# A wait ahead of the gathers of the final sum: until the last chunk of the last expert's weights is in SBUF

## Chip, cores and metric

The kernel runs on one core of one Trainium2 chip. The metric is the device time of one execution in microseconds (us); lower is better. Engines are named as in the profile: PE is TensorE's matmuls and PEld its weight loads, DVE is VectorE, ACT ScalarE, POOL GpSimd, SP SyncE.

## What is computed

One layer of a diffusion backbone on 384 tokens (128 context tokens, 256 latent tokens, D_MODEL 1024): a token mixer, then a mixture of 32 experts in which each token goes to four of them, then the final RMSNorm. The part that the change touches is the end of the routed layer and its sum:

```python
def routed_ffn(h, lp):                       # h: 384 x 1024, TOP_K = 4, 32 experts
    logits = (h @ lp["w_router"] + lp["b_router"]).astype(jnp.float32)
    top_val, top_idx = lax.top_k(logits, TOP_K)
    gates = jax.nn.softmax(top_val, axis=-1)
    ...
    def run_block(args):
        xb, e = args
        hb = xb @ w1[e] + b1[e]
        glu, lin = jnp.split(hb, 2, axis=-1)
        glu = jnp.minimum(glu, SWIGLU_LIMIT)
        lin = jnp.clip(lin, -SWIGLU_LIMIT, SWIGLU_LIMIT)
        act = glu * jax.nn.sigmoid(SWIGLU_ALPHA * glu) * (lin + 1.0)
        return act @ w2[e] + b2[e]
    ys = lax.map(run_block, (xs, block_e)).reshape(cap, d_model)
    return jnp.zeros_like(h).at[slot_t].add(ys * slot_g[:, None].astype(ys.dtype))

x = x + g2 * routed_ffn(h.reshape(B * T, D), lp).reshape(B, T, D)
y_prompt, y_sample = rmsnorm(x_ctx, norm_f), rmsnorm(x_lat, norm_f)
```

Everything is float32.

## The kernel before, in words

The program is written by hand, engine by engine: each engine has one list of instructions (`@block.sync`, `@block.gpsimd`, `@block.tensor`, `@block.scalar`, `@block.vector`), which it runs in the order written, and counting semaphores tie the lists together. Compute instructions add 1 to a semaphore and a DMA adds 16 when it has landed.

**Expert stage.** The tokens of each expert are cut into blocks of HB = 64 rows; here there are 39 blocks, one iteration each on PE, ACT, DVE and POOL, and the last of them is number `last_it` and belongs to expert 31. An expert's weights are 12 MB, in WC = 12 chunks of 1 MB: chunks 0 to 7 from `w_moe_in`, 8 to 11 from `w_moe_out`. SP issues them (line 569), expert after expert, each as soon as its buffer is free, and each chunk position c has a semaphore of its own, `s_es[c]`, which has reached 16·(e+1) when chunk c of expert e is in. Chunks 0 to 3 land in four staging buffers (two in `ring`, two in `work`), from which DVE copies them on (line 1852); chunks 4 to 7 (tile `work`) and 8 to 11 (tile `ring`) are multiplied where they land. PE multiplies in order (all matmuls have line 689): chunks 0 to 7, then, after the activation on DVE and ACT, chunks 8 to 11. At the end of every block but the last, ACT takes the 64 x 1024 result out of PSUM bank 2 and writes it to the DRAM tensor `rows_d` with two DMAs (line 1393), which count on semaphore `yo`.

**Last block.** Its result stays in PSUM. During it, ACT loads the norm gains and the modulation rows (lines 1366 to 1372; the tiles `smallw`, `first`, `work`; semaphore `cons3`).

**The gathers.** After its share of the blocks POOL waits until `rows_d` is written (`yo`, line 670), and until DVE has copied the last block's chunks 0 to 3 out of the staging buffers (`stg`, line 672), runs a tiny operation to hold its place (line 673), and issues 12 indirect DMAs (line 678). Each gathers 128 rows of 4 KB from `rows_d`, one per token, by the index column `dest[:, n]`: numbers 0 to 3 for token tile 0 (into `ring`), 4 to 7 for tile 1 (into `work`), 8 to 11 for tile 2 (into `zbuf`, after PE has multiplied chunks 0 to 3, lines 676 and 677). The semaphore `s_yg[j]` has reached 64 when tile j's four gathers have landed.

**The sum.** DVE's list after the last block (lines 1896 to 1911) is: `gathered(0)`, `gathered(1)`, two products of the last block's rows with the modulation gate (`ysc`, line 1901, which wait for PE's last multiplication and for the rows that ACT loads), `gathered(2)`, then `summed(j)`, `mean_square(j)` and `final_norm(j)` for the three tiles. `gathered(j)` waits for `s_yg[j]`, scales tile j's first gathered rows by the gate (line 1874) and adds the other three (line 1876):

```python
            def gathered(j):
                ve.wait_ge(s_yg[j], 16 * TOPK)
                L(ts(facc[j], facc[j], early[:, j, 0:1], None, M))
                for k in range(1, TOPK):
                    L(stt(facc[j], ygat[TOPK * j + k], early[:, j, k:k + 1], facc[j], M, A_))
```

PE puts the residual x1 into six banks after its last expert chunk (12 matmuls on `ky` and `ident`), and adds the last block's rows when `ysc` is there (12 matmuls on `work`, 64 rows). `summed(j)` adds a bank to tile j, ACT squares it, POOL takes the root (line 683), DVE scales (line 1894), and SP stores the tile (line 597).

Of the kernel before, what the change touches and what calls it, by code (L numbers as in the profile page):

```python
# [39 lines left out]
NE = 32  # L40
# [41 lines left out]
WC = W1C + W2C  # L82
# [60 lines left out]
def build(nc, a, o):  # L143
    ctx = ExitStack()
    with ctx:
# [46 lines left out]
        def at(buf, start, *shape, rows=P):  # L192
            n = int(np.prod(shape))
            v = buf[0:rows, start:start + n]
            if len(shape) == 1:
                return v
            names = "abcd"[:len(shape)]
            return v.rearrange(f"p ({' '.join(names)}) -> p {' '.join(names)}",
                               **{names[i]: shape[i] for i in range(len(shape))})
# [141 lines left out]
        s_es = [sem(f"s_es{i}") for i in range(WC)]  # L341
# [261 lines left out]
        @block.gpsimd  # L603
        def _(gp):
            gp.memset(at(ky, 0, D), 0.0).then_inc(S["gpn"], 1)
            gp.memset(half[:, :], -0.5).then_inc(S["gpn"], 1)
            gp.wait_ge(S["gpn"], 2)
            rs = ALU.pow
            for j in range(NT):
                gp.wait_ge(S["ssq"], j + 1)  # L610
                gp.tensor_tensor(stat[:, 8 + j:9 + j], stat[:, 4 + j:5 + j], half[:, 0:1], rs).then_inc(S["rstd"], 1)
            for j in range(NT):
                gp.wait_ge(S["anorm"], j + 1)
                gp.tensor_tensor(stat[:, 36:46], stat[:, 26:36], half[:, 0:10], rs).then_inc(S["arstd"], 1)  # L614
            for j in range(NT):
                gp.wait_ge(S["kkss"], j + 1)
                gp.tensor_tensor(stat[:, 16:24], stat[:, 8:16], half[:, 0:8], rs).then_inc(S["kkr"], 1)

            def rest_of_bias(i):
                rows = slice((0, 2 * NE)[i], QMAX)  # L620
                gp.wait_ge(S["kkr"], NT + i + 2)
                gp.wait_ge(S["b3d"], (1, 4)[i])
                gp.tensor_tensor(bias32[rows, :], bias32[rows, :], b3[rows, :], ALU.subtract).then_inc(S["b3d"], 1)  # L623

            for j in range(NT):
                gp.wait_ge(S["kkss"], NT + j + 1)
                if j == 2:
                    gp.wait_ge(S["b3d"], 2)
                gp.tensor_tensor(stat[:, 16:24], stat[:, 8:16], half[:, 0:8], rs).then_inc(S["kkr"], 1)
                if j:  # L630
                    rest_of_bias(j - 1)
            gp.wait_ge(S["b3d"], 5)
            for j in range(NT):
                gp.wait_ge(S["ssq"], NT + j + 1)
                gp.tensor_tensor(stat[:, 8 + j:9 + j], stat[:, 4 + j:5 + j], half[:, 0:1], rs).then_inc(S["rstd"], 1)

            def gather_rows():
                gp.indirect_dma_start(xg, None, h2_d.rearrange("t (h n) -> (t h) n", h=2), bass.IndirectOffsetOnAxis(ap=slots[:, 0:1], axis=0))\
                  .then_inc(S["xgd"], 16)

            def gather_first():
                gp.wait_ge(S["idxc"], 1)
                gp.wait_ge(S["h2out"], 16 * NT)
                gp.tensor_tensor(half[:, 12:13], half[:, 13:14], half[:, 13:14], ALU.mult).then_inc(S["gpn"], 1)
                gather_rows()

            def gather_listed(it):
                gp.wait_ge(S["idxc"], 2)
                gp.wait_ge(S["xgd"], 16 * it + 16)
                gp.wait_ge(S["gpn"], 3 * it + 3)  # L650
                gp.tensor_tensor(half[:, 12:13], half[:, 13:14], half[:, 13:14], ALU.mult).then_inc(S["gpn"], 1)  # L651
                gp.tensor_copy(slots[:, 0:1], lists[:, bass.ds(it + 1, 1)]).then_inc(S["gpn"], 1)
                gp.wait_ge(S["gpn"], 3 * it + 5)
                gp.tensor_tensor(half[:, 14:15], half[:, 13:14], half[:, 13:14], ALU.mult).then_inc(S["gpn"], 1)
                gather_rows()

            gather_first()
            gp.wait_ge(S["routeq"], 8)
            last_it = gp.value_load(tab[0:1, LAST:LAST + 1], min_val=NE - 1, max_val=NBMAX - 1)

            def block_of(it, last):
                if not last:
                    gp.wait_ge(S["xtm"], it + 1)
                    gather_listed(it)

            with gp.Fori(0, last_it) as it:
                block_of(it, False)
            block_of(last_it, True)

            gp.wait_ge(S["yo"], 32 * last_it + 32)  # L670
            gp.wait_ge(S["gpn"], 3 * last_it + 3)
            gp.wait_ge(S["stg"], NST * last_it + 2 * NST)
            gp.tensor_tensor(half[:, 12:13], half[:, 13:14], half[:, 13:14], ALU.mult)
            for n in range(NT * TOPK):
                if n == 2 * NST:
                    gp.wait_ge(S["mult"], WC * last_it + (NST + ZQ_ALL))
                    gp.tensor_tensor(half[:, 15:16], half[:, 13:14], half[:, 13:14], ALU.mult)
                gp.indirect_dma_start(ygat[n], None, rows_d,
                                      bass.IndirectOffsetOnAxis(ap=dest[:, n:n + 1], axis=0))\
                  .then_inc(s_yg[n // TOPK], 16)  # L680
            for j in range(NT):
                gp.wait_ge(S["ssq"], 2 * NT + j + 1)
                gp.tensor_tensor(stat[:, 8 + j:9 + j], stat[:, 4 + j:5 + j], half[:, 0:1], rs).then_inc(S["rstd"], 1)
# [1256 lines left out]
```

## Time and profile before

| | us |
|---|---|
| median of 3 runs | 1818.67 |
| the three runs | 1815.39, 1818.67, 1831.9 |
| the profiled execution | 1815.35 |
| its span, first to last instruction | 1813.5 |
| mean granted TensorE clock in it | 0.926 of full |

The profile is of one execution of its own, so its times are set against 1815.35 us. Stretches are in microseconds from the span's start. In the chain of waits each row is a start, a length, and the work, DMA or queue that the end of the program waited for at that point. In a timeline a row is one instruction or several of a kind: start, time from its start to the end of the last, engine, line, operation, tiles written and read, count, and in brackets how long the engine was idle before it and what ended that. A POOL row of a gather shows the making of the DMA's descriptors, not the moving of its data. "DMA" in a row of stretches is the mean busy share of the core's 16 DMA engines. Queue q1 is SP's, q10 is ACT's and q0 is POOL's.

### The profile page before, as it was taken

What the parts mean: (1) busy time and instruction counts of PE and PEld (TensorE: products, weight loads), DVE (VectorE), ACT (ScalarE), POOL (GpSimd) and SP (SyncE); (2) the same over time, 40 slices, a digit from 0 to 9 for tenths busy, and PEclk for the clock granted to TensorE, in tenths of its full rate; (3) what the DMA queues carried; (4) which work ended last, traced back from release to release, by engine and by line L of the source; (5) the groups of instructions that cost most, each with busy time, mean ns of one, the idle gap of its engine ahead of it and who ended that gap; (6) DMA issues with size and microseconds to landing.
All of it is one profiled execution on the core that took longest, in us unless ns stands there. A gap on an engine that the chain in (4) does not pass through costs nothing.

```text
span 1813.5 us, 28729 instructions
## 1 busy us (share of the span) xinstructions
PE 1540.9 (85%) x11145; PEld 749.4 (41%) x11146; DVE 702.4 (39%) x1093; ACT 260.1 (14%) x508; POOL 109.0 (6%) x194
## 2 busy tenths in 40 slices
PE   2699959598998996999997878999888889878974
PEld 0588825497895453333332222233222233222321
DVE  1433255777676445333322222233222232222316
ACT  0233313202212100111110101011101011001101
POOL 0000010100002100000000000000000000000020
PEclk8799968699998985999999998999999999999988
DMA  8534472300006462987799999978999989999895
GB/s 340 206 103 158 172 304 91 141 4 8 3 4 193 168 236 104 395 352 287 287 421 422 421 422 422 377 300 365 422 421 422 421 334 419 421 422 406 366 412 229
DMA packets 98524, 516.90 MB, mean 285 GB/s; under 512 B 13880, under 2 KB 16200, under 8 KB 45752
## 3 DMA queue, kind: packets, MB, share of 16 engines
q1 hardware_dynamic: 81928, 480.88, 65.8%
q10 hardware_dynamic: 11680, 18.49, 2.8%
q0 software_dynamic: 4848, 16.52, 2.5%
q8 instruction: 56, 0.92, 0.2%
q14 instruction: 12, 0.10, 0.0%
HBM read 493.12 MB, written 22.72 MB: 284 GB/s over the span
## 4 chain that ended last, share of the span: by engine, by line
PE 53%; DMA 31%; DVE 9%; issue 3%; POOL 2%; ACT 1%; SPq 0%; DVEq 0%; ACTq 0%; POOLq 0%
PE bank L689 51%; DMA work<-w_moe_in 26%; PE bank L696 2%; DMA work<-rows_d,dest 1%; DMA ring<-w_ada 1%; DVE work L1863 1%; DVE work L1597 1%; DMA work<-mods_d 1%; DMA work<-b_moe_out 1%; DVE work L1864 1%; DVE work L1606 0%; DMA rows_d<-work 0%; DVE work L1690 0%; POOL work L623 0%; POOL stat L614 0%
## 5 line engine op out<-in xcount | busy, mean ns | idle before, releaser
L689 PE MATMUL bank<-work 64*64 64x64 f32 (+3 forms) x5468 | 486.2, 324 | 79.1 <-DMA work<-w_moe_in 72.9
L689 PE MATMUL bank<-ring,work 128*64 128x512 f32 (+1 forms) x1440 | 364.2, 598 | 11.7 <-ACT work L1175 5.7
L689 PEld LDWEIGHTS bank<-work 64*64 64x64 f32 (+2 forms) x5468 | 240.0, 139 | 315.3 <-issue 161.8
L689 PE MATMUL bank<-zbuf,work 128*64 128x512 f32 (+2 forms) x1560 | 267.5, 451 | 25.0 <-DVE zbuf L1852 24.8
L689 PEld LDWEIGHTS bank<-ring,work 128*64 128x64 f32 (+1 forms) x1440 | 123.1, 145 | 220.5 <-issue 205.8
L1175 ACT ACTIVATE work<-bank 128x512 f32<-128x512 f32 (+3 forms) x227 | 112.7, 514 | 635.5 <-PE bank L689 344.9
L1857 DVE TENSOR_SCALAR work<-bank 128x512 f32<-128x512 f32 x39 | 27.0, 692 | 452.2 <-PE bank L689 452.2
L689 PEld LDWEIGHTS bank<-zbuf,work 128*64 128x64 f32 (+2 forms) x1560 | 110.4, 142 | 173.0 <-issue 106.4
L689 PE MATMUL bank<-parts 128*128 128x512 f32 (+1 forms) x720 | 158.0, 382 | 3.4 <-DVE parts L420 3.4
L696 PE MATMUL bank<-ident,work 128*128 128x128 f32 (+2 forms) x407 | 83.0, 322 | 73.2 <-DVE work L1443 21.7
L689 PEld LDWEIGHTS bank<-parts 128*128 128x128 f32 x720 | 131.5, 191 | 29.9 <-issue 3.4
L1852 DVE COPY zbuf<-work 128x2048 f32<-128x2048 f32 x78 | 94.1, 1224 | 64.7 <-DMA work<-w_moe_in 62.4
L1376 ACT ACTIVATE work<-work 128x512 f32<-128x512 f32 x39 | 24.6, 630 | 564.6 <-DVE work L1857 564.6
L696 PEld LDWEIGHTS bank<-ident,work 128*128 128x128 f32 (+2 forms) x407 | 56.0, 177 | 114.3 <-DVE work L1864 33.9
L1852 DVE COPY first<-ring 128x2048 f32<-128x2048 f32 x39 | 47.9, 1227 | 125.0 <-DMA ring<-w_moe_in 104.4
L420 DVE TENSOR_TENSOR parts<-ring,parts 128x1024 fp32r<-128x1024 f32 (+1 forms) x40 | 45.7, 1146 | 103.9 <-ACT parts L415 103.9
L689 PE MATMUL bank<-first,work 128*64 128x512 f32 x312 | 75.9, 607 | 10.4 <-DVE first L1852 10.4
L651 POOL TENSOR_TENSOR half<-half 128x1 f32<-128x1 f32 x38 | 7.5, 198 | 946.0 <-PE bank L696 935.2
L1852 DVE COPY zbuf<-ring 128x2048 f32<-128x2048 f32 x39 | 47.6, 1222 | 25.2 <-DMA ring<-w_moe_in 25.2
L1863 DVE TENSOR_SCALAR work<-bank 128x256 f32<-128x256 f32 x78 | 32.8, 420 | 62.7 <-PE bank L689 62.7
L415 ACT ACTIVATE parts<-ring 128x1024 fp32r<-128x1024 f32 (+1 forms) x40 | 39.8, 999 | 102.2 <-PE bank L689 102.2
L689 PE MATMUL bank<-ring,condT 128*2 128x512 f32 x192 | 32.6, 790 | 19.2 <-DMA ring<-w_ada 18.3
(234 smaller groups left out, 890.1 us busy)
## 6 DMA issues: line engine op xcount, KB each, us to landing
work<-w_moe_in SPq DMA_DIRECT2D x192, 1024.0 KB, 21.5
ring<-w_moe_out SPq DMA_DIRECT2D x128, 1024.0 KB, 23.3
ring<-w_moe_in SPq DMA_DIRECT2D x64, 1024.0 KB, 22.1
ring<-w_ada SPq DMA_DIRECT2D x12, 2048.0 KB, 8.6
ring<-w_in SPq DMA_DIRECT2D x9, 2048.0 KB, 8.1
rows_d<-work ACTq DMA_DIRECT2D x76, 128.0 KB, 6.6
rows_d<-ky SPq DMA_DIRECT2D x11, 512.0 KB, 15.0
ring<-w_out SPq DMA_DIRECT2D x2, 2048.0 KB, 12.9
```

The source lines that it names most:

```text
L415: nc.scalar.activation(zpart(t, 0, n), z_quarter(t), ACT.Copy).then_inc(S["hi"], 1)
L420: eng.tensor_tensor(zpart(t, 1, n), z_quarter(t), zpart(t, 0, n), ALU.subtract)\
L651: gp.tensor_tensor(half[:, 12:13], half[:, 13:14], half[:, 13:14], ALU.mult).then_inc(S["gpn"], 1)
L689: return pe.matmul(out, l, r, start=start, stop=stop)
L696: return pe.transpose(out, src, ident[0:n, 0:n])
L1175: cp = lambda out, src, scale=1.0: sc.activation(out, src, ACT.Copy, scale=scale)
L1376: sc.activation(th, gl, ACT.Tanh, scale=ALPHA / 2).then_inc(S["thd"], 1)
L1597: tt(dst, bk(d, 2 * par + i).rearrange("p (c n) -> p c n", c=2), gramm[:, d:d + 1, :].broadcast_to([P, 2, 4 * HC]), M).then_inc(S["am"], 1)
L1852: cp(slot[c], stage[c]).then_inc(S["stg"], 1)
L1857: ts(gl, B[0], LIMIT, None, ALU.min).then_inc(S["thd"], 1)
L1863: LL(ts(uu[:, seg], B[1][:, seg], LIMIT, -LIMIT, ALU.min, ALU.max))
L1864: stt(act[:, seg], uu[:, seg], 1.0, gg[:, seg], A_, M).then_inc(S["actd"], 1)
```

## The change

One wait is added to POOL's list, between the waits of line 672 and the tiny operation behind them: POOL goes on only when chunk 11 of expert 31 has landed. `WC` is 12, `NE` is 32, so the wait is for `s_es[11]` at 512, its final value. Nothing else is touched, and all later lines stand one further down.

```diff
@@ -670,6 +670,7 @@
             gp.wait_ge(S["yo"], 32 * last_it + 32)
             gp.wait_ge(S["gpn"], 3 * last_it + 3)
             gp.wait_ge(S["stg"], NST * last_it + 2 * NST)
+            gp.wait_ge(s_es[WC - 1], 16 * NE)
             gp.tensor_tensor(half[:, 12:13], half[:, 13:14], half[:, 13:14], ALU.mult)
             for n in range(NT * TOPK):
                 if n == 2 * NST:
```

POOL's list from the end of its blocks to the last gather, before the change, with the semaphores that an instruction waits for in brackets (`s_stg`: staging buffers copied; `s_mult`: chunks multiplied):

```order
L671 ISA [waits s_yo]
L672 ISA [waits s_gpn]
L673 TENSOR_TENSOR half<-half 128x1 [waits s_stg]
L678 DMA ring<-rows_d,dest 128x1024 x4
L678 DMA work<-rows_d,dest 128x1024 x4
L676 ISA
L677 TENSOR_TENSOR half<-half 128x1 [waits s_mult]
L678 DMA zbuf<-rows_d,dest 128x1024 x4
```

The same place on POOL with the change (`s_es11`: chunk 11 of an expert landed):

```order
L671 ISA [waits s_yo]
L672 ISA [waits s_gpn]
L674 TENSOR_TENSOR half<-half 128x1 [waits s_es11,s_stg]
L679 DMA ring<-rows_d,dest 128x1024 x4
L679 DMA work<-rows_d,dest 128x1024 x4
L677 ISA
L678 TENSOR_TENSOR half<-half 128x1 [waits s_mult]
L679 DMA zbuf<-rows_d,dest 128x1024 x4
```

No instruction has moved, on this or on another engine; all 12 gathers stand behind the new wait, and nothing but POOL's three root operations of the final norm stands behind the gathers.

## Rows read from the trace of the kernel before

**Rows 1.** The page: the chain that ended last, by engine and by line.

```profile
PE 53%; DMA 31%; DVE 9%; issue 3%; POOL 2%; ACT 1%; SPq 0%; DVEq 0%; ACTq 0%; POOLq 0%
```

**Rows 2.** Chain of waits from 1740 us to the end: start, length, what.

```profile
1743.87 6.98 DMA rows_d<-work
...
1750.88 0.04 POOLq L671
...
1760.56 26.88 DMA work<-rows_d,dest
...
1787.54 0.77 DVE work L1874
...
1792.38 1.29 DVE work L1901 x2
1793.66 0.67 DVE zbuf L1874
```

**Rows 3.** Timeline of POOL, 1750 us to the end.

```profile
1751.79 0.98 POOL L678 DMA_INDIRECT ring<-rows_d,dest  x1 [0.50 <-issue]
...
1755.56 0.94 POOL L678 DMA_INDIRECT ring<-rows_d,dest  x1 [0.30 <-issue]
...
1760.56 0.95 POOL L678 DMA_INDIRECT work<-rows_d,dest  x1 [0.30 <-issue]
...
1765.67 0.94 POOL L678 DMA_INDIRECT zbuf<-rows_d,dest  x1 [0.30 <-issue]
1803.65 1.48 POOL L683 TENSOR_TENSOR stat<-stat,half 128x1 f32<-128x1 f32 x1 [37.04 <-DVE stat L1889]
```

**Rows 4.** Timeline of PE and DVE, 1751 to 1800 us: last expert's chunks, then the sum.

```profile
1765.64 6.02 PE L689 MATMUL bank<-work 128*64 128x512 f32 x20 [3.03 <-DMA work<-w_moe_in]
1773.88 1.94 PE L689 MATMUL bank<-ring,work 128*64 128x512 f32 x8
1776.76 0.75 DVE L1874 TENSOR_SCALAR ring<-ring,work 128x1024 f32<-128x1024 f32 x1 [3.37 <-DMA ring<-rows_d,dest]
1777.55 3.93 DVE L1876 SCALAR_TENSOR_TENSOR ring<-ring,work 128x1024 f32<-128x1024 f32 x3
1783.49 1.94 PE L689 MATMUL bank<-ring,work 128*64 128x512 f32 x8 [1.73 <-DMA ring<-w_moe_out]
1785.36 5.42 PE L689 MATMUL bank<-ky,ident 128*128 128x512 f32 x12
1787.54 0.75 DVE L1874 TENSOR_SCALAR work<-work 128x1024 f32<-128x1024 f32 x1 [6.06 <-DMA work<-rows_d,dest]
1793.72 2.85 PE L689 MATMUL bank<-work 64*128 64x512 f32 x12 [2.94 <-DVE work L1901]
1799.67 1.29 DVE L1881 TENSOR_TENSOR ring<-bank,ring 128x512 f32<-128x512 f32 x2
```

**Rows 5.** DMA queues, 1751 to 1783 us: packets, MB, share of 16 engines.

```profile
q1 hardware_dynamic: 1008, 7.28, 58.9%
q0 software_dynamic: 882, 3.23, 26.4%
q10 hardware_dynamic: 724, 1.98, 16.5%
```

**Rows 6.** Busy time by stretch: PE, PEld, DVE, ACT, POOL, clock, DMA share, GB/s.

```profile
1720.00:1730.00 10.00, 10.00 (x48) 3.21 (x46) 0.35 (x1) 0.00 (x0) 0.00 (x0) 1.00 1.01 421
1755.00:1760.00 5.00, 1.98 (x4) 0.29 (x4) 0.00 (x0) 0.00 (x0) 3.78 (x5) 0.51 1.04 404
1783.50:1787.50 4.00, 4.00 (x13) 1.53 (x14) 0.00 (x0) 0.00 (x0) 0.00 (x0) 1.00 1.01 405
1790.00:1791.00 1.00, 0.78 (x2) 0.00 (x0) 0.96 (x2) 0.00 (x0) 0.00 (x0) 1.00 0.49 193
```

**Rows 7.** The row gathers of line 638, 690 to 715 us: issue to landing.

```profile
DMA to landing us min/median/max: 3.3/3.4/3.5
```

**Rows 8.** Timelines of POOL and DVE, 694 and 706 us: POOL beside a DVE operation.

```profile
694.11 1.18 POOL L638 DMA_INDIRECT zbuf<-h_d,slots  x1 [0.18 <-issue]
...
706.65 0.79 POOL L654 TENSOR_TENSOR half<-half 128x1 f32<-128x1 f32 x1
...
706.43 0.96 DVE L1840 TENSOR_TENSOR zbuf<-zbuf,gate 128x768 f32<-128x768 f32 x1
```

**Rows 9.** Line 654 on POOL over the whole span: duration in ns, min/median/max.

```profile
L654 POOL TENSOR_TENSOR half<-half x38: 192/192/790, 706.7 to 1710.6; 128x1 f32<-128x1 f32 x38
```

## The prediction, made before the changed kernel ran

> **What bounds the kernel now.** I read the page first, for what the whole chain is made of: 53% of it is PE and 31% is DMA [rows 1]. The change concerns the last 60 us, so the shares of the whole say little and the end of the chain of waits says more [rows 2]: the write of `rows_d` lands at 1750.88, POOL issues eight gathers, the eighth (issued at 1760.56) lands 26.88 us later, at 1787.44, and from 1787.54 DVE works without a hole worth naming (`gathered(1)`, the two products of line 1901 at 1792.38, `gathered(2)` at 1793.6, the sums). So the end of the program is set by one event: the landing of gathers 4 to 7. The last weights are not on that chain. PE takes the last chunk at 1783.49, after a wait for its DMA, and is through with it at 1785.4 [rows 4], and what it produces is first needed at 1792.38 [rows 2].
>
> Next the DMA engines. From 1720 to 1730 us, with next to nothing but weights to move, they are full at 421 GB/s; from 1755 to 1760, with the gathers among them, full at 404; from 1783.5 to 1787.5, when only gathers are left, full at 405; they go idle half way through 1790 to 1791 [rows 6]. Weights and gathers thus share one full resource until 1790.5 us. Of the 32 us from 1751 to 1783 the gathers took a share of 26.4, the weights 58.9 and ACT's small loads 16.5, which add to 101.8 [rows 5].
>
> **The change, part by part.** It adds one wait; it removes and reorders nothing. Queued behind it on POOL are the 12 gathers and the three roots of the final norm; the roots are not due before 1803.65 [rows 3]. For the gathers waits DVE alone.
>
> *Weights.* POOL now stands still from 1750.88 until chunk 11 has landed. That happened at 1783.5 [rows 4], but beside gathers. Two ways to move it: by time, the gathers' 26.4 of 101.8 parts of 32 us are 8.3 us, so chunk 11 lands at 1775.2. By bytes, the other two queues moved 7.28 + 1.98 = 9.26 MB, at the 421 GB/s of the pure stretch 22.0 us from 1751, with 0.2 for the last half microsecond 1773.2. I take the middle, T = 1774.3, and keep both ends. That gain is worth nothing in itself, since the weights are not on the chain. PE follows: it needed 8.24 us from chunk 7 (1765.64) to the first multiplication of chunk 8 (1773.88) and 1.94 us a chunk after that [rows 4]; however little of that moves, `ysc` has PE's part no later than the 1785.4 of before, and it is wanted at about 1793.
>
> *Gathers.* From the release to the first descriptor work POOL took 1751.79 - 1750.88 = 0.91 us, to that of the fourth 4.7, of the eighth 9.7, of the twelfth 14.8 [rows 2, 3]; one every 1.25 us. From a start of that kind to the landing the nearest rows are the row gathers at 690 to 715 us, with DMA engines that have nothing else: 3.4 us for half the bytes [rows 7]; the other 0.26 MB at 405 GB/s add 0.6, so 4.0. Moving 12 x 0.524 MB at 405 GB/s takes 15.5 us, which is what twelve issues take anyway (14.8), so the pace is the same by either. Tile 0's gathers land at T + 8.7 = 1783.0, tile 1's at T + 13.7 = 1788.0, tile 2's at T + 18.8 = 1793.1.
>
> *DVE.* `gathered(0)` runs from 1783.0 for 4.7 us (1776.76 to 1781.48 before [rows 4]), to 1787.7, so it is just out of the way. `gathered(1)` starts at 1788.05 against 1787.54: +0.5 us. Line 1901 follows at 1792.9, `gathered(2)` could start at 1794.1, and tile 2 is there at 1793.1. So the rest keeps its length and the end moves by +0.5 us; with T at 1773.2 by -0.6, with T at 1775.2 by +1.4.
>
> *POOL beside DVE.* This is new: before, every gather was issued by 1766.6, when DVE did little; now the eighth to twelfth are issued (from T + 9.7 = 1784.0) while `gathered(0)` and `gathered(1)` keep DVE busy, with operations that read two tiles of SBUF. What such an operation does to POOL is seen once: line 654's tiny operation takes 192 ns as a rule and 790 once [rows 9], and that once it began 0.22 us after DVE's line 1840 (two SBUF inputs, 0.96 us) and ended 0.05 us behind it [rows 8]. A gather beside small DVE operations took 1.18 us for its descriptors, against 0.95 here [rows 8, 3]. No row shows a gather beside a long DVE operation. The low bound is nothing. The high bound: each of the five misses one 1.29 us operation, so tile 1 lands 1.3 us later and tile 2 at 1793.1 + 6.5 = 1799.6, where `gathered(2)` started at 1793.6: +6.0 us. Since POOL's rhythm (1.25) is nearly DVE's (1.31), I expect one miss and then step: the eighth gather is held from 1784.0 to the end of an operation at about 1785.1; the first miss of the mean length, half of 1.3, is 0.7 us on tile 1. I take +0.7.
>
> The Trainium skill, page "SBUF — State Buffer", section "Who interferes with whom", says that a VectorE instruction with two SBUF inputs contends with a GpSimd instruction that reads SBUF, and that one in a two-port mode contends with any, the later one waiting for the whole instruction. The held operation of line 654 agrees. The page infers that descriptor making needs only the write side, by which the adding operations would not hold a gather and only the three 0.75 us scalings could: the sum would then be about +0.5 to +1.2. If the index read counts as a read of SBUF, it is nearer the +6. No run so far shows which.
>
> *Clock.* When PE starved between 1755 and 1760 its granted clock was 0.51 [rows 6], the lower of its two levels, 1.2 GHz. PE will now idle some 10 us before the 12 matmuls that took 2.85 us at 1793.72, where it had idled 2.94 [rows 4]; at half the clock they take 5.7. `summed` adds bank after bank from 1799.67 on, one tile per 2.5 us, so 4 us of cover stand in front of the first bank and more in front of the last: nothing.
>
> **Sum.** +0.5 + 0.7 = +1.2 us: 1816.5 against the profiled execution's 1815.35, and 1819.9 against the median of 1818.67. Two of the four executions known lie at 1815.4 and one at 1831.9, so the median stands a little high; I give a number between the two, 1818.5.
>
> **The rivals.**
> (a) *The weights don't come sooner* (they keep the pace they had and the gathers' share is just lost). Then T = 1783.5, tile 1 lands at 1783.5 + 13.7 = 1797.2, 9.7 us after 1787.5: 1825.1, or 1828.4 on the median. It decides from the point where the weights' queue does not take up what the gathers leave. Against it: 421 GB/s with weights almost alone [rows 6]. For it: ACT's small loads and the landing receipts of a queue with few chunks left (nothing is issued behind chunk 11) might not fill 16 engines.
> The Trainium skill, "DMA: Bandwidth & Descriptors", section "Issuing engines are not separate DMA queues", says that all issuers' DMAs run on the same 16 engines and interleave; by that rule (a) gets next to no chance and T is 1773 to 1775.
> (b) *POOL starves beside DVE*: +0.5 + 5.5 = +6.0 as worked out, 1821.4 (1824.7 on the median). For it the held operation, against it the gather beside small operations, which lost 0.2 us.
> (c) *Faster*: T = 1773.2 and no interference, -0.6 us: 1814.7. `gathered(0)` then ends at 1786.6, so even gathers that land faster give no more than -0.9 with that T.
> (d) *The wait does nothing*, because it is met when POOL comes to it: 0 us, 1815.35. Against it: POOL comes at 1750.88, and PE still waited for that DMA at 1783.5 [rows 2, 4].
> (e) *Slower by over 1%*, over 18 us: (a) and (b) together are 9.7 + 5.5 = 15.2, so this needs gathers that move at well under the 405 GB/s of [rows 6] once alone.
>
> **Chances.** The forecast, -0.3 to +3 us, 0.70; (a) 0.10; (b), +3 to +6, 0.11; (c) 0.04; (d) 0.02; (e) 0.03. A measurement of this kernel tells about 1% (18 us) from no change: all but (e) and stray runs lie within it, so slower 0.04, faster 0.02, same 0.94. The range goes from (c) less 2 us of spread, 1813, to (a) on the median, 1829; that holds the bounds of T (-0.6 to +1.4) and of POOL (0 to 5.5).
>
> **What would show it.** Right: POOL's first gather some 0.9 us behind the last chunk's landing, that landing at 1773 to 1775 by this trace's clock; the DMA engines full until then, then idle for some 2 us, then at about 405 GB/s to 1793; DVE's idle time ahead of `gathered(1)`, 6.06 us before [rows 4], under 1 us; the chain running through chunk 11's DMA, POOL's issues and tile 1's landing. Wrong: chunk 11 at 1783 (a); descriptor rows of over 1.2 us and a wait of DVE for tile 2 (b); gathers at another pace alone than the 405 GB/s they had at the end.

## The result, and the profile after

Twenty executions of each kernel, interleaved, give a median of 1832.1 us for the changed kernel (1820.1 to 1842.2) and 1821.2 us for the kernel before (1808.2 to 1842.0); the ratio is 1.0067, with a 95% interval of 1.0039 to 1.0095. The change costs time: some 12 us by this ratio. The prediction was 1818.5 us, 1813 to 1829, with a chance of 0.94 that no change of 1% would be seen. The profiled execution took 1840.38 us, with a span of 1838.5 at a mean granted clock of 0.908.

The ratio leaves out executions over 1.5% above the fastest of their own kernel, a bound of about 1835 us for the kernel before and 1847 for the changed one, and so takes more long executions from the one than from the other; over all forty the means are 1822.1 and 1832.2 us, 10.1 apart.

The two profiles differ by 25.0 us in span, and most of that is not where the change is. The last write of `rows_d` is issued well before the new wait matters. I call the start of that issue the anchor, and the time from it to the end of the span the tail. The row of ACT that issues it, in the kernel before:

```profile
1743.23 1.14 ACTq L1393 DMA_DIRECT2D rows_d<-work  x2
```

and in the changed kernel:

```profile
1763.87 1.14 ACTq L1394 DMA_DIRECT2D rows_d<-work  x2
```

So the changed kernel was 20.6 us late before its tail began, and the tail was 1838.5 - 1763.87 = 74.6 us against 1813.5 - 1743.23 = 70.3: +4.4. Of the 20.6, 20.3 are there already at the start of the expert stage: POOL's first DMA of line 638 starts at 694.11 us in the one and at 714.41 in the other. Where they came from is seen in the stretches of the token mixer (columns as in [rows 6]), in the kernel before:

```profile
275.00:300.00 25.00, 25.00 (x129) 13.37 (x126) 12.88 (x37) 7.12 (x24) 0.00 (x0) 0.82 0.31 119
300.00:325.00 25.00, 19.73 (x122) 12.57 (x121) 15.36 (x40) 7.74 (x25) 1.64 (x1) 0.86 0.13 36
```

and in the changed kernel:

```profile
275.00:300.00 25.00, 25.00 (x86) 13.79 (x86) 9.88 (x27) 5.63 (x18) 0.00 (x0) 0.50 0.28 111
300.00:325.00 25.00, 25.00 (x83) 12.98 (x76) 7.00 (x21) 5.08 (x16) 0.00 (x0) 0.50 0.00 1
```

In the same 50 us PE did 169 matmuls instead of 251, without an idle moment, at a granted clock of 0.50, the lower of its two levels (1.2 GHz), instead of 0.82 and 0.86. The program there is the same in both. Whether the change has a part in it is what the first experiments ask.

Now the tail. The chain of waits of the changed kernel, which answers to [rows 2]:

```profile
1763.16 33.10 DMA ring<-w_moe_out
...
1796.39 0.19 POOL half L674
...
1797.09 0.97 POOL ring L679
...
1805.87 6.57 DMA work<-rows_d,dest
...
1812.54 0.77 DVE work L1875
...
1817.38 1.29 DVE work L1902 x2
1818.67 0.67 DVE zbuf L1875
```

The last weight (tile `ring`) is now on the chain; it lands at 1796.26, 32.4 us after the anchor, where the last chunk of before was taken at 40.3. From there the chain goes through POOL's issues and the landing of the eighth gather, 6.57 us after its issue, to the same DVE operations as before. `gathered(1)` starts 48.7 us after the anchor instead of 44.3.

The timelines of POOL and PE/DVE, which answer to [rows 3, 4]:

```profile
1793.14 7.09 PE L690 MATMUL bank<-ring,work 128*64 128x512 f32 x32
1797.09 0.97 POOL L679 DMA_INDIRECT ring<-rows_d,dest  x1 [0.50 <-issue]
1800.87 0.95 POOL L679 DMA_INDIRECT ring<-rows_d,dest  x1 [0.30 <-issue]
1807.25 0.75 DVE L1875 TENSOR_SCALAR ring<-ring,work 128x1024 f32<-128x1024 f32 x1 [14.60 <-DMA ring<-rows_d,dest]
1808.04 3.92 DVE L1877 SCALAR_TENSOR_TENSOR ring<-ring,work 128x1024 f32<-128x1024 f32 x3
1808.47 1.67 POOL L679 DMA_INDIRECT zbuf<-rows_d,dest  x1 [0.30 <-issue]
1812.54 0.76 DVE L1875 TENSOR_SCALAR work<-work 128x1024 f32<-128x1024 f32 x1 [0.57 <-DMA work<-rows_d,dest]
1818.72 5.07 PE L690 MATMUL bank<-work 64*128 64x512 f32 x12 [13.15 <-DVE work L1902]
```

One gather of twelve was held: its descriptors took 1.67 us instead of 0.95, and it began while DVE's first two-input addition (1808.04 to 1809.33) was running. It belongs to tile 2, for which nobody waited. PE's final 12 matmuls took 5.07 us instead of 2.85 after 13 us of idleness, and `summed` did not wait for them.

The queues from 1771.6 us (the anchor plus 7.7, the place of [rows 5]) until chunk 11 has landed:

```profile
q1 hardware_dynamic: 1007, 7.27, 76.2%
q10 hardware_dynamic: 725, 1.99, 21.7%
```

The weights moved the same 7.27 MB as in [rows 5] in 24.7 us instead of 32. And the DMA engines after that, by stretches:

```profile
1795.00:1797.00 2.00, 2.00 (x12) 0.62 (x10) 0.00 (x0) 0.00 (x0) 0.19 (x1) 1.00 0.16 61
1797.00:1799.00 2.00, 2.00 (x12) 0.71 (x10) 0.00 (x0) 0.00 (x0) 1.61 (x2) 1.00 0.23 29
1799.00:1801.00 2.00, 2.00 (x8) 0.63 (x5) 0.00 (x0) 0.00 (x0) 1.39 (x3) 1.00 0.80 262
1801.00:1804.00 3.00, 3.00 (x8) 1.33 (x7) 0.00 (x0) 0.00 (x0) 2.39 (x3) 1.00 0.96 320
1804.00:1806.00 2.00, 1.57 (x4) 0.38 (x2) 0.00 (x0) 0.00 (x0) 1.39 (x3) 1.00 0.92 297
1806.00:1808.00 2.00, 0.00 (x0) 0.00 (x0) 0.75 (x1) 0.00 (x0) 1.83 (x3) 1.00 0.98 344
1808.00:1810.00 2.00, 0.00 (x0) 0.00 (x0) 1.93 (x3) 0.00 (x0) 1.70 (x2) 0.90 1.01 401
1810.00:1812.00 2.00, 0.00 (x0) 0.00 (x0) 1.93 (x2) 0.00 (x0) 1.39 (x3) 0.50 1.02 416
```

This is the view to read twice. The last column is GB/s, the one ahead of it the busy share. After the last weight the engines stand empty for some three microseconds. When the gathers come, the engines are nearly fully "busy" (0.92 to 0.98 from 1801 on) and yet move only 262 to 344 GB/s, from 1799 to 1808; only from 1808 on do they reach the 401 to 416 that matches the 405 of [rows 6], for gathers late in their stream.

What that does to the single gathers is seen in their times from issue to landing. The first takes 4.4 us, the second 5.2, the third 5.5, the fourth 6.4, and the fifth to the eighth 6.5 to 6.6. So each falls behind the one ahead of it until the fourth, although POOL issues one every 1.25 us as forecast.

### The profile page after: what moved, and what is told of

The parts are those of the page before. It is cut to its first block, busy times and chain, and to the rows that moved or that the text cites. A ratio compares the mean times of both kernels' runs of the same rounds, so it can differ in the third digit from the quotient of the medians.

```text
span 1838.5 us, 28730 instructions
## 1 busy us (share of the span) xinstructions
PE 1568.3 (85%) x11145; PEld 762.7 (41%) x11146; DVE 703.4 (38%) x1093; ACT 261.2 (14%) x508; POOL 109.9 (6%) x194
## 4 chain that ended last, share of the span: by engine, by line
PE 53%; DMA 32%; DVE 9%; issue 3%; POOL 2%; ACT 1%; SPq 0%; DVEq 0%; ACTq 0%; POOLq 0%
PE bank L690 50%; DMA work<-w_moe_in 27%; PE bank L697 2%; DMA ring<-w_moe_out 2%; DMA ring<-w_ada 1%; DVE work L1864 1%; DVE work L1598 1%; DMA work<-mods_d 1%; DMA work<-b_moe_out 1%; DVE work L1865 0%; DVE work L1607 0%; DMA work<-rows_d,dest 0%; DVE work L1691 0%; POOL work L623 0%; POOL stat L614 0%
## 5 line engine op out<-in xcount | busy, mean ns | idle before, releaser
L690 PE MATMUL bank<-work 64*64 64x64 f32 (+3 forms) x5468 | 504.9, 329 | 87.4 <-DMA work<-w_moe_in 71.1
L690 PEld LDWEIGHTS bank<-work 64*64 64x64 f32 (+2 forms) x5468 | 246.4, 140 | 334.7 <-issue 175.4
L690 PEld LDWEIGHTS bank<-zbuf,work 128*64 128x64 f32 (+2 forms) x1560 | 115.0, 146 | 168.4 <-issue 108.6
L420 DVE TENSOR_TENSOR parts<-ring,parts 128x1024 fp32r<-128x1024 f32 (+1 forms) x40 | 45.7, 1145 | 104.0 <-ACT parts L415 104.0
L690 PE MATMUL bank<-ring,condT 128*2 128x512 f32 x192 | 36.8, 881 | 19.4 <-DMA ring<-w_ada 18.5
```

The source lines that it names most:

```text
L420: eng.tensor_tensor(zpart(t, 1, n), z_quarter(t), zpart(t, 0, n), ALU.subtract)\
L690: return pe.matmul(out, l, r, start=start, stop=stop)
```

## The experiments

Tail times are from the issue of the last write of `rows_d` in each kernel's own profile; "first row gather" is the place of POOL's first DMA of line 638, at the start of the expert stage, and shows how long everything ahead of the experts took.

| kernel | first row gather at | tail | first of the 12 gathers | gathered(0) | gathered(1) | gathered(2) |
|---|---|---|---|---|---|---|
| before | 694.1 | 70.3 | 8.6 | 33.5 | 44.3 | 50.4 |
| aa | 725.1 | 70.0 | 8.6 | 33.3 | 44.0 | 50.0 |
| placebo | 705.1 | 69.9 | 8.7 | 33.4 | 44.0 | 50.0 |
| changed | 714.4 | 74.6 | 33.2 | 43.4 | 48.7 | 54.7 |
| again | 714.0 | 74.7 | 33.3 | 43.4 | 48.7 | 54.8 |
| again2 | 693.5 | 74.9 | 33.5 | 43.6 | 48.7 | 55.0 |
| chunk10 | 700.2 | 72.6 | 31.0 | 41.3 | 46.5 | 52.7 |
| chunk9 | 704.7 | 70.1 | 28.5 | 38.8 | 44.0 | 50.2 |
| chunk7 | 694.3 | 70.2 | 20.8 | 38.9 | 44.1 | 50.2 |
| late8 | 724.0 | 70.8 | 8.6 | 33.4 | 44.3 | 50.8 |
| late4 | 723.2 | 74.5 | 8.6 | 33.2 | 48.6 | 54.6 |
| zbuf_first | 720.8 | 80.6 | 34.5 | 49.5 | 54.6 | 60.7 |
| ysc_early | 704.6 | 69.1 | 8.5 | 33.4 | 44.0 | 49.1 |
| after_ysc_early | 719.4 | 73.6 | 33.3 | 43.3 | 48.4 | 53.6 |

The profiled executions of `aa`, `late8` and `late4` are among the longest of their kernels. Their extra time lies ahead of the anchor: `aa` has its first row gather 31 us later than the kernel before, and the same tail.

### Is it the wait, and is it only the tail?

`again` and `again2` are the changed kernel, unedited. Their expectations:

> The changed kernel once more, 5 rounds beside the kernel before. Measured from the last write of rows_d (ACT, line 1394) to the end, its profile was 4.4 us longer than before's; the other 20.6 us of the two profiles' difference lie ahead of that point, most of it at 275 to 350 us, where TensorE's granted clock was 0.50 instead of 0.82 to 0.86. Theory A (the tail costs some 4 us, the rest is the spread of that clock from execution to execution): ratio near 1.002, tail again +4.4, and the stretch 275 to 350 us long or short in either kernel. Theory B (the added wait also makes the early stretch slow more often): ratio near 1.007 and the early stretch slow again.

> The changed kernel a third time. Both profiles so far show a tail of +4.4 us, while the ratios were 1.0067 and 1.0058 (+12 and +11 us), and 59 executions of before, the placebo and before's copy against 32 of the changed kernel differ by 8 us in their means. Theory A (only the tail; the rest is the spread of the early stretch's clock and the way in which long executions are left out): a mean over all executions at +3 to +7 us. Theory B (something else of 4 to 6 us, outside the tail): +8 to +12 again, and then in this profile a stretch ahead of the tail that is longer than before's.

Measured: `again` 1834.6 us median of 12, ratio 1.0058 (1.0024 to 1.0092), tail 74.7; `again2` 1829.0 of 12, ratio 1.0037 (0.9997 to 1.0077), tail 74.9. The mean of `again2` was 2.2 us above that of the kernel before in the executions beside it, below what either theory asked for. In the profile of `again2` the first row gather stands at 693.5 us, as early as in the kernel before, and the tail is the long one all the same.

The placebo:

```diff
-            gp.wait_ge(s_es[WC - 1], 16 * NE)
+            gp.wait_ge(s_es[WC - 1], 16 * (NE - 1))
```

> The same added wait at the same place, but for chunk 11 of expert 30 (16 * 31), which has landed long before POOL comes to it; so the same instructions, and no delay. Theory A: ratio 1.000 and a tail of before's length. Theory B (the additional instruction itself does something to the early stretch): +8 us, ratio near 1.004, with before's tail.

Measured: ratio 0.999 (0.9959 to 1.0021), tail 69.9. The instruction costs nothing, the waiting does.

`aa` is the kernel before, unedited.

> The kernel before against itself, to see what 5 rounds can tell: ratio 1.000, interval some 0.4% wide. Spans of single executions between 1808 and 1842 us, with the early stretch (275 to 350 us) at either clock.

Measured: ratio 0.9991 (0.9962 to 1.0019), tail 70.0, with one execution of 2491.9 us that stands alone and is left out everywhere here. Its profile is the one with the longest early part of all (first row gather at 725.1 us), 31 us later than in the first profile of the same program. So the early part is long or short in either kernel.

Over all executions, the kernel before, `aa` and `placebo` have a mean of 1825.0 us (137 executions, standard error 0.8), the changed kernel 1831.5 (44, standard error 1.2): +6.5, give or take 1.4. The tail explains 4.7 (mean of three, 74.7, less the mean of three, 70.1). But that pools executions of several groups. Against the executions of the kernel before that were interleaved with it, the changed kernel's mean lay 10.1, 9.6 and 2.2 us higher, and that of `after_ysc_early` (below), which has the same wait and a tail 3.5 us longer than before's, 0.6 us lower. Less the tails, these four differences have a weighted mean of +1.6, give or take 1.4, which chance may well leave.

The profiles say more. From the first row gather to the anchor the kernel before, `aa` and `placebo` take 1049.6 us in the mean and the three of the changed kernel 1050.1; ahead of the first row gather it is 708.1 and 707.3. So outside the tail the profiles are no longer with the wait than without. I take theory A as borne out; what the first twenty executions of each kernel show beyond the tail, 6 to 8 us, has no place in any profile, and a second effect of 2 or 3 us isn't excluded by the executions alone.

### What in the late start costs?

Three kernels wait for an earlier chunk; each is this edit of the changed kernel with another number. "Theory D" in the expectations is that a stream of gathers which meets empty engines moves slowly at first, whatever it gathers.

```diff
-            gp.wait_ge(s_es[WC - 1], 16 * NE)
+            gp.wait_ge(s_es[W1C - 1], 16 * NE)    # chunk 7; also with 9, with 10
```

> The wait is for chunk 7 of expert 31 instead of chunk 11, so POOL starts some 12 us after before's start and 13 to 14 us ahead of the changed kernel's, while chunks 8 to 11 are still moving. If what costs is the empty time and the slow start of the DMA engines behind the last weight, all of it goes: the gathers queue beside weights, tile 1 lands within 1 us of before and the tail is 70.3 +- 1. Rival (what costs is the late start as such, 4.4 us for 26 us of delay, so pro rata): tail 72.2 to 72.5.

> The wait is for chunk 9 of expert 31: POOL starts with two more chunks (2 MB, 5 us) still to move. All times from the issue of the last write of rows_d; before: gathered(1) starts at 44.3, tail 70.0 to 70.3. Theory D (what costs is that the gathers meet empty engines): two chunks bridge most of it; the eighth gather is issued at about 37.1, and with the 6.2 us from issue to landing that late gathers show it lands at 43.3, ahead of before's 44.2, so gathered(1) starts at 44.0 to 44.5 and the tail is 70 to 70.7. Rival (any delay past the start of the last chunks costs pro rata, 0 at chunk 7 and 4.5 at chunk 11): tail 72.3.

> The wait is for chunk 10, one chunk (2.5 us) ahead of the changed kernel's. Theory D: the eighth gather is issued at 39.6 and lands at 45.8, gathered(1) starts at 45.9 to 46.3, tail 71.6 to 72.3: half of the changed kernel's loss with a quarter of chunk 7's lead. Rival (pro rata): tail 73.5.

Measured: chunk7 tail 70.2 (ratio 1.0008, 0.9968 to 1.0048), chunk9 70.1 (0.9997, 0.9960 to 1.0035), chunk10 72.6 (1.0024, 0.9979 to 1.0069). POOL was delayed by 12, 20, 22 and 25 us in the four kernels and the tail grew by 0, 0, 2.5 and 4.6. It is flat up to chunk 9, and from there nearly one for one: 2.5 us of later release and 2.5 of tail to chunk10, 2.2 and 2.1 from there to the changed kernel. In all three of these `gathered(1)` starts 6.6 to 6.7 us after the eighth gather's issue, so the tails alone would also fit a fixed delay of that size behind a release that comes too late; the stretches tell the cases apart. In chunk9 the engines never run dry, and the gathers wait behind weights that move at full rate (GB/s last):

```profile
1785.00:1788.00 3.00, 3.00 (x16) 1.00 (x14) 0.00 (x0) 0.00 (x0) 2.39 (x3) 1.00 1.00 399
1788.00:1791.00 3.00, 3.00 (x14) 0.97 (x11) 0.00 (x0) 0.00 (x0) 2.23 (x3) 1.00 1.02 407
```

In chunk10 they do, and the slow start is there:

```profile
1780.00:1782.00 2.00, 2.00 (x12) 0.64 (x10) 0.00 (x0) 0.00 (x0) 1.47 (x2) 1.00 0.41 76
1782.00:1785.00 3.00, 3.00 (x16) 0.78 (x12) 0.00 (x0) 0.00 (x0) 2.31 (x3) 1.00 0.90 309
1785.00:1788.00 3.00, 3.00 (x9) 1.44 (x8) 0.00 (x0) 0.00 (x0) 2.39 (x3) 1.00 0.93 339
```

For chunk10 I had expected at most 72.3; it missed by 0.3.

Is the slow start one of the place in the stream, or of what gathers 0 to 7 read and write?

```diff
-            for n in range(NT * TOPK):
+            for n in [8, 9, 10, 11, 0, 1, 2, 3, 4, 5, 6, 7]:
```

> The changed kernel with the gathers issued in the order 8 to 11, 0 to 3, 4 to 7 (so all behind chunk 11). In the changed kernel the first eight gathers moved at some 300 GB/s with the DMA engines nearly full, the last at 416. Theory D (a stream of gathers that meets empty engines is slow at first, whatever it gathers): the first ten us run at 200 to 330 GB/s again, now with the gathers into zbuf, and the first group takes some 6 us from its last issue to landing. Theory C (the gathers into ring and work are slow by their rows or their destination): the first five us run at 400 GB/s or more, the slow stretch comes behind. Either way tile 0 and tile 1 land 5.1 us later than in the changed kernel, so the tail from the last write of rows_d is about 5 us longer than its 74.6, some 79.7.

Measured: tail 80.6, 0.9 more than expected (the first gather was itself 1.3 us later than in the changed kernel), ratio 1.0168 (1.0094 to 1.0242, two executions). The stretches:

```profile
1805.00:1807.00 2.00, 2.00 (x9) 0.58 (x6) 0.00 (x0) 0.00 (x0) 1.23 (x3) 1.00 0.00 0
1807.00:1809.00 2.00, 2.00 (x6) 0.93 (x5) 0.00 (x0) 0.00 (x0) 1.70 (x2) 1.00 0.73 213
1809.00:1812.00 3.00, 3.00 (x7) 0.97 (x6) 0.00 (x0) 0.00 (x0) 2.09 (x4) 1.00 0.95 313
1812.00:1814.00 2.00, 0.00 (x0) 0.00 (x0) 0.00 (x0) 0.00 (x0) 1.70 (x2) 1.00 0.91 289
1814.00:1816.00 2.00, 0.00 (x0) 0.00 (x0) 0.00 (x0) 0.00 (x0) 1.39 (x3) 0.67 1.01 373
1816.00:1818.00 2.00, 0.00 (x0) 0.00 (x0) 0.00 (x0) 0.00 (x0) 1.51 (x2) 0.50 1.01 401
1818.00:1820.00 2.00, 0.00 (x0) 0.00 (x0) 0.00 (x0) 0.00 (x0) 1.57 (x2) 0.50 1.03 420
```

Now the gathers into `zbuf` are the slow ones, and the later ones into `ring` and `work` move at 401 to 420. So it goes by place in the stream. It also isn't POOL's making of descriptors, which goes on while 401 to 420 GB/s are moved (column of POOL, 1.51 and 1.57), nor PE's reading, which ends ahead of the 289 GB/s stretch. Whether it is the shortness of the queue in front of the engines or something else in them no run shows.

The same start with another group of gathers:

```diff
+                if n == NST:
+                    gp.wait_ge(s_es[WC - 1], 16 * NE)
+                    gp.tensor_tensor(half[:, 11:12], half[:, 13:14], half[:, 13:14], ALU.mult)
                 if n == 2 * NST:
```

(the added wait of the change is taken out).

> Gathers 0 to 3 are issued as before, 4 to 11 wait for chunk 11 (a one-element operation of POOL on another column of half holds their place). Gathers 0 to 3 land as before (gathered(0) at 33.5); of the 8.3 us that gathers had of the engines ahead of chunk 11 some 5 remain, so it lands at about 37. Theory D (each late stream starts slowly, whichever gathers it has): the fourth late gather is issued at 37 + 4.7 = 41.7 and lands 6.4 us later, as the fourth of the changed kernel did: gathered(1) starts at 48.1, tail 73.9. Rival (the slow landing comes from eight gathers being queued, as I had 4.0 us): gathered(1) at 45.7, tail 71.5.

Measured: `gathered(1)` at 48.6, tail 74.5, which are theory D's 48.1 and 73.9 and not the 45.7 and 71.5 of my 4.0 us. In part that is luck: POOL went on at 38.6 instead of 37, the fourth late gather was issued at 42.7 instead of 41.7, and it took 5.9 us to `gathered(1)` instead of 6.4. The 5.9 lies nearer to 6.4 than to 4.0. Holding back eight gathers cost as much as holding back twelve here, because chunk 11 landed some 6 us later and four gathers fewer were in front. (Two executions, no ratio.)

### Versions that might be better

```diff
                 if n == 2 * NST:
                     gp.wait_ge(S["mult"], WC * last_it + (NST + ZQ_ALL))
+                    gp.wait_ge(s_es[WC - 1], 16 * NE)
```

(again without the change's own wait).

> The wait for chunk 11 stands ahead of gathers 8 to 11 only; gathers 0 to 7 are issued as before. If the tail is set by the landing of gathers 4 to 7 alone, taking 8 to 11 out of their way lets them land sooner: before, about 2.1 MB of gathers 8 to 11 shared the engines with them. Theory A: tile 1 lands some 2 to 3 us sooner, chunk 11 at about 2 us sooner, gathers 8 to 11 land about 10 us behind chunk 11, near 1792 by before's clock, just in time: tail -1 to -2 us. Rival (late gathers move slowly whenever few are in flight): gathers 8 to 11 land at 1794 or later and gathered(2) waits for them: tail 0 to +2 us.

Measured: tail 70.8, ratio 1.0002 (0.9973 to 1.0030); `gathered(1)` at 44.3, and PE takes chunk 11 at 40.2, against 44.3 and 40.3 before. The expectation was wrong in its first half: tile 1 lands no sooner, and neither does chunk 11. I infer that gathers 8 to 11, issued behind 4 to 7 in POOL's own queue, had moved nothing before those were through, and so had taken nothing from them or from the weights. The kernel before agrees: up to 1783 us POOL's queue had moved 3.23 MB [rows 5], less than the 4.19 MB of the first eight. And they land late enough that `gathered(2)` waits (0.4 us by the table of waits), which is the rival's "0 to +2".

The other edit is on DVE, in the kernel before (`ysc_early`) and in the changed one (`after_ysc_early`, ahead of both gathered calls):

```diff
             gathered(0)
-            gathered(1)
             ve.wait_ge(S["cons3"], 16 * (NCONS3 + NCONS4 + 7))
             ve.wait_ge(S["mult"], WC * last_it + (WC + ZQ_ALL))
             for i in range(2):
                 tt(ysc[i], B[2], g2h[i], M).then_inc(S["yc"], 1)
+            gathered(1)
```

> The kernel before (no added wait) with the two products of line 1901 ahead of gathered(1) on DVE, in the 6.1 us in which DVE waits for tile 1; PE is through with the last chunk at 1785.4, tile 1 lands at 1787.4. If the chain from the landing of tile 1 on is DVE's own work and nothing else, as the chain of waits says, the tail gets shorter by the products' 1.3 us: 69.0 against 70.3. It needs tile 2 (DMA engines idle from 1790.5) by 1792.3. Rival: PE's products or tile 2 are late, 0. On the whole execution 1.3 us is 0.07%, below what rounds can tell.

> The changed kernel with the two products of line 1902 ahead of gathered(0) on DVE. PE is through with chunk 11 at 36.3 and DVE idles until 43.4, so they cost nothing there; the chain from tile 1's landing (48.6) is DVE's own work, which is 1.3 us shorter: tail 73.4 against 74.6 to 74.9, if tile 2 (DMA engines idle some 52.8 after the anchor) is there by 53.4. In the mean over all executions it should lie 3 to 4 us above before; with something else in the changed kernel that costs 4 to 6 us (theory B) 8 to 9 us.

Measured: `ysc_early` tail 69.1, 0.9 to 1.2 less than before's three; ratio 0.9994 (0.9961 to 1.0027). `after_ysc_early` tail 73.6, 1.2 less than the changed kernel's; ratio 0.9986 (0.9952 to 1.0020), its mean 0.6 us below that of before in the executions beside it, where +3 to +4 was expected: the spread of whole executions again, since its profiled tail is longer than before's by 3.5. DVE in `ysc_early`:

```profile
1795.56 1.29 DVE L1900 TENSOR_TENSOR work<-bank,work 128x512 f32<-128x512 f32 x2 [3.90 <-PE bank L689]
1797.57 0.75 DVE L1874 TENSOR_SCALAR work<-work 128x1024 f32<-128x1024 f32 x1 [0.72 <-DMA work<-rows_d,dest]
1802.68 0.75 DVE L1874 TENSOR_SCALAR zbuf<-zbuf,work 128x1024 f32<-128x1024 f32 x1 [0.39 <-DMA zbuf<-rows_d,dest]
```

The products fit into the hole, and the gain stops at 0.9 to 1.2 instead of 1.3 because tile 2 is then 0.39 us late. `ysc_early` has the shortest tail of all kernels; its mean lay 5.7 us below that of the kernel before beside it, five times what the tail gained, which is one more measure of how whole executions scatter.

## Why the prediction was wrong, step by step

- *The end of the program is set by the landing of gathers 4 to 7, and the weights are not on the chain.* Right for the kernel before; `after_ysc_early` and `ysc_early`, which shorten DVE's work behind it, shorten the tail.
- *Chunk 11 lands sooner, T = 1774.3.* The gain was there: 7.9 us instead of the 9.2 predicted. By before's clock T was 1743.23 + 32.39 = 1775.6, 1.3 us later than taken and 0.4 beyond the late bound. The estimate by time was the better one; the one by bytes took the 421 GB/s of pure weights, while weights mixed with ACT's small loads moved 9.26 MB in 24.7 us, 376 GB/s.
- *From the issue of a gather on idle engines to its landing 4.0 us, and from there the engines keep POOL's pace.* This step failed, and in its second half above all. The first gather took 4.4 us, near the forecast. The eighth took 6.57, +2.6 us: "the pace is the same by either" (issues at 419 GB/s, engines at 405) was wrong for the first nine microseconds, when the engines moved 262 to 344 GB/s. The 405 belonged to gathers late in their stream. By an estimate from these rows, 4.4 us and then seven more gathers of 0.524 MB at 405 GB/s would have landed the eighth 13.5 us behind the first issue; it took 15.35, so the slow start cost 1.9 us and the first landing 0.4.
- *POOL beside DVE, +0.7.* The mechanism was right: one gather held by 0.7 us, by an operation with two SBUF inputs; that the size matches is chance in part, since it hangs on where in that operation the gather began. That happened to the tenth gather and not to the eighth, since tile 0 came later too, and so it cost nothing on the chain. The Trainium skill, page "SBUF — State Buffer", section "Who interferes with whom", infers that descriptor making needs only the write side, by which such additions should not stop it. In the changed kernel a gather that began in one took 1.67 us against 0.95, which fits the same section's rule for a GpSimd instruction that reads SBUF; the measurement decides, and which read it is no run shows.
- *Clock.* Right: 5.07 us instead of 2.85, begun at a granted clock of 0.50, the lower level, and covered.
- *Sum.* +0.5 (T = 1774.3) plus 1.3 for chunk 11 plus 2.6 for the landing makes +4.4, which is what the tail of the changed profile shows; I had +1.2, of which the 0.7 for POOL did not come. Rival (a), +9.7, was wrong in its mechanism, (b) in its size.
- *The range.* The mis-sized terms of the tail alone would not have left it: +3.2 us on 1818.5 is 1821.7. I set the range around three executions, 1815 to 1832, and took what they spread over as all there is; twenty executions of before span 34 us. Of the 13.6 us between forecast and median, 3.2 are the tail. Another 3.9 are that 1818.5 less my +1.2 stands for a kernel before of 1817.3, whose median came out at 1821.2. The other 6.5 are in no profiled tail; the later executions speak for chance, and show no cause. The cost of the wait is 4.4 to 4.7 us by the tails (0.25%), within the 1% that I gave 0.94, but not nothing.

## What to carry to other kernels

Holding small transfers back "until the big ones are through" frees bandwidth, but it pays twice: here the engines stood empty for some 3 us from the last weight's bytes to the first gather's, and the fresh stream started below its full rate, some 2 us more. Release it while some transfers are still queued (here two 1 MB chunks sufficed, one did not), and ask first whether the transfer that gets the freed bandwidth is on the chain at all. For effects of a few microseconds measure from an anchor near the change: the tail told 4.4 us reproducibly to 0.3 in three profiles, where whole executions scatter by 30.

## What was not expected of the hardware

- DMA engines at a busy share of 0.90 to 0.98 moved 289 to 344 GB/s: a share near 1 is no proof of full rate. It was seen in the changed kernel, with another wait in chunk10 and with other gathers in `zbuf_first`.
- Gathers that stand behind others of POOL's queue cost SP's queue nothing in the one case here: `late8` held 2 MB of them back, and PE took chunk 11 at 40.2 us after the anchor instead of 40.3.
- The same instructions ahead of the expert stage took from 693.5 us to 725.1 us in fourteen profiles, in step with TensorE's granted clock between 250 and 375 us. The three at 693.5 to 694.3 (before, chunk7, again2) had 0.82 or 0.83 from 275 to 300; the five at 719.4 to 725.1 had 0.50 for all of 250 to 350. That is a spread of 31 us, against 4.4 for this change. Here it stayed at 0.50 for all of 275 to 350 us in `aa`, the kernel before:

```profile
275.00:300.00 25.00, 25.00 (x81) 12.54 (x80) 10.43 (x28) 5.69 (x18) 0.00 (x0) 0.50 0.40 158
300.00:325.00 25.00, 25.00 (x87) 13.52 (x86) 7.88 (x24) 5.27 (x16) 0.00 (x0) 0.50 0.00 0
325.00:350.00 25.00, 23.51 (x87) 15.17 (x88) 11.17 (x27) 5.69 (x18) 0.00 (x0) 0.50 0.01 2
```

Why the clock rises early in one execution and late in another was not tried.
